# Two row products ahead of 21 products of the first eighth, at the beginning of a two-layer hybrid model

## The reference, cut to what matters

```python
cond = jax.nn.silu(c)
for layer in range(DEPTH):
    mod = cond @ ada_w[layer] + ada_b[layer]
    shift, scale, gate = jnp.split(mod[:, None, :], 3, axis=-1)
    h = rms_norm(x, norm_w[layer]) * (1.0 + scale) + shift
    ...
        y = even_mixer(h, ev_w_in[i], ev_w_out[i], ...)   # starts with proj = h @ w_in
    x = x + gate * y
return rms_norm(x, final_norm_w)
```

## Time and profile before

| | us |
|---|---|
| median of 3 runs | 1794.38 (1793.57 to 1797.4) |
| profiled execution: its time | 1793.83 |
| profiled execution: its span, first to last instruction | 1792.0 |
| the beginning, to the last row product | about 123 of it |

### The profile page before, as it was taken

The page is one execution under the profiler, slowest core; times in us unless marked ns, Lnnn a source line. Parts: engine busy times, 40 slices in busy tenths (PEclk is TensorE's granted clock), DMA queues, the critical chain, the costliest instruction groups (busy, mean ns, idle before and its releaser), DMA issues.

```text
span 1792.0 us, 29072 instructions
## 1 busy us (share of the span) xinstructions
PE 1757.9 (98%) x11736; PEld 1408.6 (79%) x11736; DVE 1206.8 (67%) x2412; ACT 679.4 (38%) x1505; POOL 7.2 (0%) x14
## 2 busy tenths in 40 slices
PE   7899999999999999999999999999999999999997
PEld 3668787888878787888877888788888888888887
DVE  3876677675858686765857766747777777783333
ACT  4335344343435353443535322423332333253221
POOL 0000000000000000000000000000000000000001
PEclk9999999999999999999999999999999999999999
DMA  9983323333333433233232877343333333324332
GB/s 375 384 331 138 128 106 124 118 137 117 120 110 118 146 108 125 106 112 141 107 119 102 277 241 242 116 147 142 112 121 134 130 118 112 142 83 153 118 119 105
DMA packets 56085, 268.08 MB, mean 150 GB/s; under 512 B 6280, under 2 KB 7944, under 8 KB 35728
## 3 DMA queue, kind: packets, MB, share of 16 engines
q1 hardware_dynamic: 55952, 266.23, 41.7%
HBM read 257.28 MB, written 8.93 MB: 149 GB/s over the span
## 4 chain that ended last, share of the span: by engine, by line
PE 94%; DMA 3%; DVE 2%; SPq 0%; ACT 0%; issue 0%; DVEq 0%; ACTq 0%
PE psum L700 26%; PE psum L702 25%; PE psum L701 25%; DMA ada_x<-in_ada_first 2%; PE psum L739 1%; PE psum L1162 1%; PE psum L740 1%; PE psum L973 1%; PE psum L741 1%; PE psum L992 1%; PE psum L1189 1%; PE psum L717 1%; PE psum L1175 1%; PE psum L851 1%; PE psum L872 1%; PE psum L983 0%
## 5 line engine op out<-in xcount | busy, mean ns | idle before, releaser
L700 PE MATMUL psum<-mov_hi,w_hi 128*128 128x512 f32 x1952 | 789.6, 404 | 0.9 <-DVE w_lo L1724 0.6
L702 PE MATMUL psum<-mov_hi,w_lo 128*128 128x512 f32 x1952 | 763.0, 391 | 0.0
L701 PE MATMUL psum<-mov_lo,w_hi 128*128 128x512 f32 x1952 | 761.8, 390 | 0.0
L700 PEld LDWEIGHTS psum<-mov_hi,w_hi 128*128 128x128 f32 x1952 | 367.1, 188 | 85.7 <-issue 11.6
L702 PEld LDWEIGHTS psum<-mov_hi,w_lo 128*128 128x128 f32 x1952 | 366.9, 188 | 79.4
L701 PEld LDWEIGHTS psum<-mov_lo,w_hi 128*128 128x128 f32 x1952 | 367.8, 188 | 67.2
L1724 DVE TENSOR_TENSOR w_lo<-w_raw,w_hi 128x512 fp32r<-128x512 f32 x504 | 336.0, 684 | 101.0 <-ACT w_hi L1306 100.4
L1306 ACT ACTIVATE w_hi<-w_raw 128x512 fp32r<-128x512 f32 x504 | 291.1, 621 | 11.5 <-PE psum L702 10.9
L1740 DVE SCALAR_TENSOR_TENSOR ada_acc<-ada_t,silu_c,ada_acc 128x512 f32<-128x512 f32 x240 | 178.6, 744 | 10.4 <-DMA ada_t<-in_ada_late 3.2
L1643 ACT ACTIVATE pr<-pr,st 128x128 f32<-128x128 f32 x128 | 49.7, 390 | 119.5 <-DVE st L2336 119.5
L1597 ACT ACTIVATE osq<-res 128x512 f32<-128x512 f32 x28 | 17.7, 633 | 203.2 <-DVE res L2254 203.1
(11 more groups left out here) (379 smaller groups left out, 1822.4 us busy)
## 6 DMA issues: line engine op xcount, KB each, us to landing
w_raw<-in_w_pack SPq DMA_DIRECT2D x126, 1024.0 KB, 4.8
ada_t<-in_ada_late SPq DMA_DIRECT2D x128, 512.0 KB, 5.6
x_in<-in_ada_first SPq DMA_DIRECT2D x14, 1024.0 KB, 8.6
w_raw<-in_w_early SPq DMA_DIRECT2D x8, 896.0 KB, 9.4
ada_t<-in_ada_first SPq DMA_DIRECT2D x7, 1024.0 KB, 7.3
ada_x<-in_ada_first SPq DMA_DIRECT2D x7, 1024.0 KB, 12.1
res<-in_x_t SPq DMA_DIRECT2D x4, 1024.0 KB, 8.3
xr<-in_x_t SPq DMA_DIRECT2D x16, 256.0 KB, 3.7
```

Of the source, the lines that this page charges most:

```text
L700: mm(PJ[r], w_hi[r][:, ks], mov_hi[:, kt], start=(j == 0), stop=False)
L701: mm(PJ[r], w_hi[r][:, ks], mov_lo[:, kt], start=False, stop=False)
L702: ins = mm(PJ[r], w_lo[r][:, ks], mov_hi[:, kt], start=False, stop=(j == KC - 1))
```

## The change

On TensorE the row products of quarters 2 and 3 of piece 2 move ahead of the 21 products of `early(0, 2)` and `early(0, 3)`, and its column products move between these two. `early` itself, for every eighth, is written in two loops: first high x high and low weight x high for all its blocks, for which it waits only until the rounded block is there, then the products with the remainder, ahead of which it now waits for that. On VectorE, for piece 2 alone, the four operations on quarter 0 of piece 3 are cut in two pairs with the two remainders between them. The rest, SyncE's order and ScalarE's among it, stays.

```diff
--- before.py
+++ after.py
@@ -732,13 +732,16 @@
                 if part == 0:
                     pe.wait_ge(wle_ok, e + 1)
                 if part % 2 == 0:
+                    pe.wait_ge(hi_ok, k + 1)
+                kt = slice(k * T, k * T + T)
+                block_cols = lambda b: slice((kk * NB_E + b) * P, (kk * NB_E + b) * P + P)
+                for b in (range(0, 4), range(4, NB_E))[part % 2]:
+                    mm(EARLY[b], w_hi[e % 2][:, block_cols(b)], mov_hi[:, kt], start=(k == 0), stop=False)
+                    mm(EARLY[b], w_lo[e % 2][:, block_cols(b)], mov_hi[:, kt], start=False, stop=False)
+                if part % 2 == 0:
                     pe.wait_ge(lo_ok, k + 1)
-                kt = slice(k * T, k * T + T)
                 for b in (range(0, 4), range(4, NB_E))[part % 2]:
-                    ks = slice((kk * NB_E + b) * P, (kk * NB_E + b) * P + P)
-                    mm(EARLY[b], w_hi[e % 2][:, ks], mov_hi[:, kt], start=(k == 0), stop=False)
-                    mm(EARLY[b], w_hi[e % 2][:, ks], mov_lo[:, kt], start=False, stop=False)
-                    ins = mm(EARLY[b], w_lo[e % 2][:, ks], mov_hi[:, kt], start=False, stop=(k == KC - 1))
+                    ins = mm(EARLY[b], w_hi[e % 2][:, block_cols(b)], mov_lo[:, kt], start=False, stop=(k == KC - 1))
@@ -763,11 +766,11 @@
             ada_products(2, 0)
             ada_products(2, 1)
-            early(0, 2)
-            early(0, 3)
             ada_products(2, 2)
             ada_products(2, 3)
+            early(0, 2)
             ada_columns(2)
+            early(0, 3)
             early(1, 0)
@@ -1781,16 +1784,16 @@
-            def early_ada(n, q):
+            def early_ada(n, q, js=range(4)):
...
-                if q == 0:
+                if js[0] == 0 and q == 0:
...
-                else:
+                elif js[0] == 0:
                     dve.wait_ge(ade_used, D_USED[n] + q)
                 dve.wait_ge(*in_piece(n, q))
-                for j in range(4):
+                for j in js:
@@ -1864,10 +1867,14 @@
-                if n + 1 < len(PIECES) and UNITS[n + 1][0] > 0:
+                if n == 2:
+                    early_ada(3, 0, range(0, 2))
+                elif n + 1 < len(PIECES) and UNITS[n + 1][0] > 0:
                     early_ada(n + 1, 0)
                 for k in ks:
                     split_lo0(k)
+                if n == 2:
+                    early_ada(3, 0, range(2, 4))
```

## The result

| | median, us | runs | against before, 95% interval |
|---|---|---|---|
| before, beside it | 1794.16 | 20 | |
| changed kernel | 1796.6 (1793.76 to 1800.83) | 20 | 1.0017 [1.0011, 1.0023] |
| the same again, later | 1798.2 (1793.36 to 1802.24) | 11 | 1.0023 [1.0013, 1.0033] |

The change costs 2.4 us, and 4.6 when it was run again (before it then stood at 1793.56).

What follows compares the result with a forecast made beforehand. It took TensorE, busy 98%, as the bound, with VectorE and transfers close behind in the beginning. -0.5 + 0.3 + 1.4 = +1.2 on 1793.83 gave 1795.0, so 1795.5 for the median; range 1792.7 to 1799.0.

Steps and rivals of the forecast that it cites:

- three chains: In the beginning, TensorE, VectorE's serial work and the transfers run close together, and the change shortens only one.
- step 7: Three thinner places on TensorE: clock falls cost nothing to 3.4 us; one fall taken, at +1.4.
- slower rival: TensorE falls cold behind the new wait, 37.9 to 41.2, and restarts cold later: +3.3 to +5.3, about 1798.7; chance 0.17.
- Step 1: Piece 2's row products: reached at 37.9, a 2.4 us transfer wait before quarter 3's, end at 42.3; idle time moved ahead.
- Step 2: Second eighth's column products start at 45.0 instead of 45.49, 12 products covering VectorE's copy of the row.
- Step 3: Second eighth's products start near 47.95 without waiting for the remainder and end at 50.7, not 54.9: gain 4.2 us.
- Step 4: Row product of piece 3's quarter 3 waits for its transfer to 54.05; gain left 1.7 us at the third eighth's columns.
- Step 5: The split adds about 1.1 us to VectorE's chain; third eighth's columns at 58.35 against 58.88, gain left 0.5 us.
- Step 6: Transfer of piece 4's quarter 1 issued at 54.5 instead of 53.99; bounds 0 and +0.5 us, +0.3 taken.
- list of signs: What the new profile should show, including piece 3's quarter 3 row product released by a transfer near 54.
- faster rival: The second eighth's waits are filled and nothing takes their place: 5.3 us go, 1789.1; chance 0.05.

Runs made afterwards that it cites:

- e1: The changed kernel with VectorE's four operations on quarter 0 of piece 3 in one go again, ahead of both remainders; median 1795.9 us, 1.0009 against before.
- e3: The changed kernel with products of zeros added in TensorE's new waits to hold the clock; median 1794.0 us, 0.9999 against before.
- e12: The kernel before with only the order of the calls on TensorE changed, without the two loops or the split; median 1792.5 us, 0.9994 against before.
- e11: The changed kernel itself, run again later for a second profile; median 1798.2 us, 1.0023 against before.
- e4: e1 with quarters 0 and 1 of piece 3 also done on TensorE as row products instead of on VectorE; median 1793.5 us, 1.0002 against before.
- e9: e4 with products of zeros ahead of the row products of quarters 2 and 3 of piece 2; median 1793.7 us, 1.0005 against before.

## Why the prediction was right, and where it wasn't

The three chains are as it put them, and its number holds. But it forecast a loss of 1.1 us on the median, and 2.4 and 4.6 came: the way and the range are right, the size is short, and that the number lies near the first median is in part luck. The term that was too small is the clock's, step 7. Both profiles show its slower rival, which had 0.17.

- *Step 1, the wait is moved.* Right: the row products end at 43.0, at half clock, against 42.3. Its place was half missed. Step 1 let (2, 2) start at 37.9 without a wait; it waits for its own transfer, to 38.60 after and to 38.5 in e1. And 37.9 is the place of an execution whose earlier fall lasts to 33, as in the profile of before: e1 comes to it at 37.8, the kernel after at 35.3, so that it stands 3.9 us in both row products' waits instead of 2.4.
- *Step 2, columns at 45.0.* 44.79 in e1 and 45.27 in e3, where the clock is full; 46.41 and 47.40 in the kernel after.
- *Step 3, no wait for the remainder.* Right: first product at 49.42, without a wait for `mov_lo`. That this is worth little shows in e12.
- *Step 4, (3, 3) has its transfer at 54 whatever TensorE does.* Right, and the best-tested step: in the 14 profiles that transfer is issued anywhere from 39.9 to 44.7 and lands between 52.5 and 54.0. (3, 3) starts between 52.7 and 54.2 in all but before (55.74), with the second eighth's columns anywhere from 42.7 to 47.4. But in the two profiles of the kernel after it isn't released by the transfer, as the prediction's list of signs has it: TensorE comes to it 0.1 and 1.2 us after the landing (53.13 and 52.95).
- *Step 5, the split adds 1.1 us to VectorE's chain, columns of the third eighth at 58.35.* The chain: 1.2. The columns: 58.61 in e3, 59.77 and 60.74 where the clock fell, later one for one with the second eighth's.
- *Step 6, +0.3 for a later issue.* Not seen. It followed the buffer of (3, 1) and not that of (3, 0), which the split frees later as well: by step 5's own numbers (4, 0) comes at 49.3 + 0.7 + 1.5 = 51.5 instead of 49.77; e3 has 51.69, the kernel after 52.85 and 53.83. The engines then stand 2.1 and 3.6 us longer than before. But TensorE's waits for transfers behind it are 1.4 and 0.9 us, against 1.4 before, so this cost it nothing that the profiles show.
- *Step 7, one fall at +1.4.* Mis-sized. Both profiles of the kernel after show two falls between 33 and 70, in the waits of (2, 2) and (2, 3) and about the end of the last wait, at the places that the slower rival names. The first makes the second eighth's columns 1.1 and 2.1 later than in e3, and the third eighth's 1.2 and 2.1; the second costs 1.73 and 3.15 on the way to (4, 2). Together that is 2.9 and 5.3 where step 7 took 1.4. The rival's columns at 60.75, its restart at 1.4 to 3.4 and its 1798.7 stand beside 60.74, 3.15 and 1798.78 in e11. In the first profile, 1798.55, it is 59.77 and 1.73, and 2.3 us come from behind the beginning. It should have had more than 0.17: e3 shows that without falls nothing is lost.
- *The faster rival* is out: the kernel after is slower, and in place of the wait of 3.9 for `mov_lo` stand waits of 3.3 and 3.2. The Trainium skill (Perfetto Trace Analysis, Optimization Strategy) would have the gap's blockers start sooner; here that took the gap away, and two others came for it.

In the table the rate from 15 to 125 and the end of the beginning go together over 14 profiles, from 374 GB/s and 155.3 to 398 GB/s and 148.0. That doesn't say which sets which: the same bytes in a beginning that is longer for another reason give a lower rate too. Where the queue is full, TensorE's waits or not, it moves 419 to 425 GB/s in the rows from 37.5 to 50. The Trainium skill (DMA: Bandwidth & Descriptors, Where 436 GB/s comes from) gives 435 GB/s for the ports of the memory on the chip; these rows come close to it. That the transfers hold (3, 3) is read from where they land; no run changed the number of bytes.

*Open:* what the upper group of e1's runs did, and why e12, with the same order on TensorE, hardly shows one; why e4's and e9's earlier columns don't show in their medians; whether the split costs where the clock falls; whether the two loops alone gain about 1 us (0.9992 and 0.9995).

## What to carry to other kernels

A wait that is moved ahead of dense products can bring a half clock with it, and each follower in the chain inherits the delay: price it as a fall in the new wait and one in the next, not as idle time alone. When an operation is moved on an engine, list every buffer whose last reader it is, and follow each transfer that comes later to an engine that waits for it: here the gap between two issues grew from 5.0 to 9.8 us and the DMA engines stood still for 2.6, yet no row product behind it waited longer. Before two profiles are compared, compare their clocks ahead of the place: here, in the same program, the fall ahead ended at 27.2 in one and at 33.0 in the other, and the wait behind it was 3.27 us and 0.68.

## What was not expected of the hardware

The clock's falls differ from one execution to the next of the same kernel. In the two profiles of the kernel after, the one around row products (2, 2) and (2, 3) lay at 37.5 to 44.3 and at 39.8 to 46.6, an earlier one at 24.0 to 27.2 and at 26.2 to 29.4, and the later one, from 949, was there once and once not. Over the first 20 runs the mean granted clock went with the time (0.991 at 1800.83, 0.996 at 1795.26; correlation -0.82), over the 11 later ones it did not (-0.03): a mean over the span doesn't say whether a fall lay where another engine waits for it.

Half clock came in the middle of a wait and not with its start. Ahead of the fall at 37.5, TensorE did row products from 33.43 to 35.33 and then stood; the granted clock still read 1.00 from 35.33 to 37.50 and 0.50 behind it. In e11 the wait of 2.23 us ahead of (2, 2) left the clock at 1.00, that row product took 1.04, and the fall came at 39.8, in the next wait of 1.46. In e1 waits of 0.68 and 1.44 in the same places left it at 1.00, and in e3 products with zeros there did. The Trainium skill (TensorE: Matmul & The Clock Gate, Loop structure matters more than you think) warns of long waits for a transfer ahead of the products; these rows agree, and the warning, which the prediction gave 0.17, was the better forecast of the two profiles.
